# Side products and evictions of a decoder layer filed between four parts of each slab, and the indexer keys filed ahead of the decays

## The reference

```python
h = rms_norm(x, attn_norm_g)
proj = h @ w_in                  # hq hf hi hg cq ak av ik iw gate_a gate_b
oa = hgrn2_mixer(hq, hf, hi, lb)           # gated recurrence, 4 heads of 128
oa = rms_norm(oa, hgrn_norm_g) * silu(hg)
cq = rms_norm(cq, q_norm_g)
aq, iq = cq @ w_uq, cq @ w_iq
ik = layer_norm(ik, idx_k_norm_g, idx_k_norm_b)
ob = dsa_mixer(aq, iq, iw, ak, av, ik, rel_bias)
mix = sigmoid(gate_a) * (oa @ w_up_hgrn) + sigmoid(gate_b) * (ob @ w_up_attn)
x = x + mix @ w_o                # then the MLP and a last RMSNorm
```

## Time and profile before

| | us |
|---|---|
| three runs | 774.33, 774.77, 776.5 |
| median | 774.77 |
| profiled execution, own time | 774.76 |
| its span in the trace | 773.0 |
| PE busy | 735.1 |
| DVE busy | 549.0 |
| ACT busy | 353.4 |
| POOL busy | 85.3 |

### The profile page before, as it was taken

The page is one execution under the profiler, slowest core; times in us unless marked ns, Lnnn a source line. Parts: engine busy times, 40 slices in busy tenths (PEclk is TensorE's granted clock), DMA queues, the critical chain, the costliest instruction groups (busy, mean ns, idle before and its releaser), DMA issues.

```text
span 773.0 us, 9939 instructions
## 1 busy us (share of the span) xinstructions
PE 735.1 (95%) x3498; PEld 608.7 (79%) x3498; DVE 549.0 (71%) x868; ACT 353.4 (46%) x571; POOL 85.3 (11%) x121
## 2 busy tenths in 40 slices
PE   5999998896998999999999999999999999999995
PEld 4788887785876788888888878878787878787884
DVE  5587997758999886434833686776869595968964
ACT  6463445465443344433321754635354444445441
POOL 5021330010001244400200100000000000000003
PEclk9999999999999999999999999999999999999998
DMA  7421221201231121112350624140505142332002
GB/s 283 158 89 56 81 82 55 83 28 54 83 109 55 56 81 56 55 54 83 119 209 27 218 81 137 55 163 24 187 6 167 50 138 79 109 109 86 23 1 109
DMA packets 20724, 71.51 MB, mean 92 GB/s; under 512 B 2344, under 2 KB 3536, under 8 KB 20688
## 3 DMA queue, kind: packets, MB, share of 16 engines
q1 hardware_dynamic: 19120, 67.88, 25.7%
q10 hardware_dynamic: 1568, 3.15, 1.2%
HBM read 68.91 MB, written 2.11 MB: 92 GB/s over the span
## 4 chain that ended last, share of the span: by engine, by line
PE 72%; DVE 17%; issue 5%; ACT 3%; DMA 1%; POOL 1%; DVEq 0%; SPq 0%; POOLq 0%; ACTq 0%
PE bank L1432 21%; PE bank L1434 21%; PE bank L1433 21%; DVE sc L1103 2%; PE bank L1655 2%; DVE small L1100 2%; DVE wlo L946 2%; DVE acc L1312 2%; PE bank L1440 1%; DVE wlo L1279 1%; PE bank L1559 1%; DVE al L1304 1%; DMA xs<-x 1%; ACT whi L860 1%; DVE sc L1090 1%
## 5 line engine op out<-in xcount | busy, mean ns | idle before, releaser
L1432 PE MATMUL bank<-hTh,whi 128*128 128x512 f32 (+1 forms) x456 | 181.1, 397 | 1.5 <-DVE hTl L966 1.5
L1433 PE MATMUL bank<-hTl,whi 128*128 128x512 f32 (+1 forms) x456 | 178.7, 392 | 0.0
L1434 PE MATMUL bank<-hTh,wlo 128*128 128x512 f32 (+1 forms) x456 | 178.6, 392 | 0.0
L1432 PEld LDWEIGHTS bank<-hTh,whi 128*128 128x128 f32 (+1 forms) x456 | 86.1, 189 | 21.2 <-issue 3.0
L946 DVE TENSOR_TENSOR wlo<-raw,whi 128x1024 fp32r<-128x1024 f32 x58 | 72.2, 1246 | 42.0 <-ACT whi L630 42.0
L1434 PEld LDWEIGHTS bank<-hTh,wlo 128*128 128x128 f32 (+1 forms) x456 | 85.9, 188 | 18.7
L1433 PEld LDWEIGHTS bank<-hTl,whi 128*128 128x128 f32 (+1 forms) x456 | 85.9, 188 | 18.2 <-issue 0.5
L1432 PE MATMUL bank<-whi,ah 128*128 128x512 f32 x196 | 77.8, 397 | 2.1 <-DVE acc L1312 2.1
L1434 PE MATMUL bank<-whi,al 128*128 128x512 f32 x196 | 76.4, 390 | 0.0
L1433 PE MATMUL bank<-wlo,ah 128*128 128x512 f32 x196 | 76.4, 390 | 0.0
L630 ACT CAST whi<-raw 128x1024 fp32r<-128x1024 f32 x58 | 60.4, 1044 | 34.7 <-PE bank L1434 34.5
(11 more groups left out here) (227 smaller groups left out, 1396.8 us busy)
## 6 DMA issues: line engine op xcount, KB each, us to landing
raw<-slabs SPq DMA_DIRECT2D x87, 512.0 KB, 3.3
br<-slabs SPq DMA_DIRECT2D x32, 512.0 KB, 3.3
xs<-x SPq DMA_DIRECT2D x4, 512.0 KB, 5.6
y<-x ACTq DMA_DIRECT2D x1, 2048.0 KB, 9.2
out<-ys SPq DMA_DIRECT2D x3, 512.0 KB, 2.6
bt<-bias_rows ACTq DMA_DIRECT2D x1, 1024.0 KB, 5.3
cst<-consts SPq DMA_DIRECT2D x1, 608.0 KB, 9.1
fg<-final_g SPq DMA_DIRECT2D x1, 512.0 KB, 7.3
```

Source lines behind the costliest of these rows:

```text
L1432: pe.matmul(dst, lh, rh, start=start, stop=False)
L1433: pe.matmul(dst, lh, rl, start=False, stop=False)
L1434: return pe.matmul(dst, ll, rh, start=False, stop=stop)
```

## The change

Each slab is cut into four parts of six matmuls, and the side steps and evictions are filed between them. `woven[n][p]` holds the steps that follow part p: the steps with PE products are spread evenly over the four parts (one goes after the third, two after the second and fourth, three after the first, third and fourth), and steps without a product stay behind the one that they follow. Evictions of part p stand ahead of these steps, for kinds by token and for iq and uq one bank in each part; `EARLY` goes. `cqT`, `kdT` and the other key steps are filed ahead of `decay_k`, `use_k` and `decay_q`, `turn` ahead of `use_q`; `ikd` and `ikh` get space of their own (197.5 and 195, which held the bias rows until they were written out), DVE's wait on `kk_done` goes, ACT waits on `scr_done` (the bias rows' write) instead, and `ikl` is made in `kdT`, not in iq's eviction.

```diff
-        ikd = place("ikd", 165, T)
-        ikh = place("ikh", 167, T, F32R)
+        ikd = place("ikd", 197.5, T)
+        ikh = place("ikh", 195, T, F32R)
...
-        file(n_de - 1, ("decay_k",))
-        file(n_de, ("put", LEVELS - 1), ("use_k",), ("decay_q",))
-        file(n_de + 1, ("use_q",), ("turn",))
         file(n_hi, ("ikT",))
         file(n_hi + 1, ("prep",))
         file(n_hi + 2, ("cqT",))
         file(n_hi + 3, ("kdT",))
+        file(n_de - 1, ("decay_k",))
+        file(n_de, ("put", LEVELS - 1), ("use_k",), ("decay_q",))
+        file(n_de + 1, ("turn",), ("use_q",))
...
-        EARLY = (n_hi + 3, n_iq, n_uq, n_hg + 3)
...
+        PARTS = 4
+        woven = {}
+        for n in range(NPLAN):
+            woven[n] = [[] for _ in range(PARTS)]
+            count = sum(s in BK for s in side[n])
+            seen, p = 0, 0
+            for s in side[n]:
+                if s in BK:
+                    p = (2 * seen + 1) * PARTS // (2 * count)
+                    seen += 1
+                woven[n][p].append(s)
...
                 hi(n + AHEAD)
-                if n in EARLY:
-                    evict(n)
-                for s in side[n]:
-                    do_side(s)
-                if n not in EARLY:
-                    evict(n)
+                for p in range(PARTS):
+                    evict(n, p)
+                    for s in woven[n][p]:
+                        do_side(s)
...
                     b, u = BK[s][2]
+                    act.wait_ge(S["scr_done"], 16)
                     act.wait_ge(free[b], u + 1)
                     act.activation(ikh[:, :], ikd[:, :], ACT.Copy).then_inc(S["ikh_done"], 1)
...
                     wait_full((b, u))
-                    dve.wait_ge(S["kk_done"], 1)
                     dve.tensor_scalar(ikd[:, :], bank[b][:, :], vec[:, V_IKG:V_IKG + 1], vec[:, V_IKB:V_IKB + 1],
                                       ALU.mult, ALU.add).then_inc(free[b], 1)
+                    dve.wait_ge(S["ikh_done"], 1)
+                    dve.tensor_tensor(ikl[:, :], ikd[:, :], ikh[:, :].bitcast(F32), ALU.subtract).then_inc(S["ikl_done"], 1)
...
-                if kind == "ua":
-                    for q, (b, u) in enumerate(tiles[n]):
-                        m = 2 * j + q
+                if kind == "ua" and p % 2:
+                    q = p // 2
+                    b, u = tiles[n][q]
+                    m = 2 * j + q
...
             for n in range(NPLAN):
-                mms(n)
-                for s in side[n]:
-                    do_side(s)
+                for p in range(PARTS):
+                    mms(n, p)
+                    for s in woven[n][p]:
+                        do_side(s)
```

## The result

The changed kernel takes 778.43 us in the median of 8 runs (777.69 to 778.8). The kernel before, run 8 times beside it, takes 775.62 us (773.92 to 777.59). The ratio is 1.0036 with a 95% interval of 1.0024 to 1.0049. I had forecast 771.6, with 766.5 to 777.5 as the range: the sign was wrong, and the time lies above the range. It lies where rival C stood, 778.5.

The account below looks back on a forecast made before the run. PE was taken to bound most stretches, DVE's queue 170 to 281 us. Terms −0.75 − 2.35 + 0.3 − 0.4 = −3.2 took 774.8 to 771.6 us, range 766.5 to 777.5.

Parts of the forecast that it names:

- rival C: Three-head slabs 29, 30, 32, 33: fourth quarter left behind ob's wait at lower clock, +1.8 each; 778.5 us; chance 0.20.
- What bounds the kernel: Whole order to 424 us: PE to 125, ACT/DVE chain to 138.5, PE to 170, DVE's queue to 281, then PE.
- Part 1: Slabs 0 to 15: side products a quarter slab earlier, +0.5 us on PE; GpSimd's price only changes bearer, 0.
- Part 2: Keys and iq, slabs 15 to 18 (120 to 148 us): later iq evictions delay PE, +1.1 us.
- Part 3: hg1 to uq (148 to 200 us): rounds earlier, −0.75 with part 2 included; DVE's slab 22 wait gone, −2.35.
- Slab 28: Start of attention: DVE arrives 3.1 us early, PE waits some 4 to 6 us instead of about 1; no price.
- Part 4: Attention, slabs 28 to 34 (234 to 281 us): slower heads and lower clock against filled gaps, +0.3 us taken.
- Part 5: 281 to 424 us, PE-bound: heads move but don't grow, one wait of 0.47 us goes, −0.4 us.
- A: Rival, 170 to 281 us: the weave fills 3/4 of DVE's gaps too; 766.5 us; chance 0.17.

Follow-up runs that it names:

- x1: Changed kernel, but in slabs 28 to 34 side products and evictions stand behind the whole slab; 771.25 us, ratio to before 0.9946.
- x3: Changed kernel with slabs 29 and 30 alone put back to their sides behind the whole slab; 775.08 us, ratio to before 0.9989.
- x5: Changed kernel with PE's idle waits in slabs 28 and 29 filled by 20 and 16 matmuls without a result; 774.76 us, ratio to before 0.9993.
- x13: x1 with ACT's wait for the last out product put back ahead of uq's first quarter; 771.17 us, ratio to before 0.9939.
- x9: Kernel before with only ACT's wait for the last out product moved to uq's third quarter of evictions; 772.34 us, ratio to before 0.9968.
- x2: Changed kernel with slab 28 alone put back to its sides behind the whole slab; 775.0 us, ratio to before 0.9994.
- x10: x5 with two more waits filled, 12 matmuls in slab 30 and 8 in slab 32; 773.31 us, ratio to before 0.9972.
- x8: Changed kernel, new key order kept, with only slabs 18 to 22 woven and all others whole; 770.29 us, ratio to before 0.9931.
- x6: x1 with slabs 16 to 18 whole too, use_k and decay_q filed behind iq's evictions; 768.27 us, ratio to before 0.9915.
- x11: x6 with only slabs 19 to 22 woven, all others whole; 768.25 us, ratio to before 0.9904.

## Why the prediction was wrong, point by point

- **What bounds the kernel**: right. DVE's lead at 200 us (3.7) is kept to 234 us without loss, and with x1's order to the end.
- **Part 1** (+0.5 on PE, 0 for GpSimd's price): slab 16 begins on PE at 120.77, before at 120.86, and PE has no idle time from 43 to 120 us. So the +0.5 did not come, nor the 121.7 from which part 2 starts. GpSimd's subtraction now falls beside `wlo` in two slabs (2.32 and 2.78 us instead of 1.25 and 1.21), and the multiplies that took 2.91 us take 1.22: the price stays in the main, with another bearer. This is also what the Trainium skill, "SBUF — State Buffer", "Who interferes with whom", would have: `wlo` too has two inputs in SBUF.
- **Part 2** (+1.1): right in nearly every step. The fourth `hV` ended at 134.8 (forecast 135.5), PE waited 2.02 us there (2.3), the last `iqs` pair ended at 144.0 (144.6), slab 19 began at 148.47 (148.6). One wait is not where I had it. I wrote that PE would reach the first indexer product at 142.0 and wait until 144.6. In this execution PE got there at 144.43 and waited for nothing, since the twelve matmuls ahead of it ran at 0.50. In the profiles of x3 and x5, whose lower stretch is half as long there, the wait is 1.22 and 1.25 us, and the product begins at 144.62 and 144.85. So the last `iqs` pair bounds it as forecast, and the lower clock only takes the wait's place. Here are the two waits of PE in the changed kernel:

```profile
134.88 0.44 PE L1439 MATMUL bank<-cqh,whi 128*128 128x384 f32 x1 [2.02 <-ACT hV L708]
...
138.32 0.77 PE L1439 MATMUL bank<-whi,hTh 128*128 128x512 f32 x1 [2.12 <-DVE iqs L1001]
```

- **Part 3** (−3.1 together): right, and a little small. The rounds began at 169.69 (169.6), `aqs` on DVE at 185.44 without a wait, the lead was 3.7. What I had missed is a second reason: I gave the gain of slab 22 to the weave, which x13 bears out, but the change also moves ACT's wait for the last `out` product, and that alone gives the gain too (x9).
- **Slab 28**: the step that failed first. I wrote that PE would wait there some 4 to 6 us, and it waited 4.8; but I put no price on it and gave no reason for that. I missed that the weave leaves 18 of the 24 matmuls behind that wait, and with them the second head (behind twelve) and the third (behind all 18), for which DVE then waits. Price 2.9 us; x2 and the table show it, x10 shows that 0.1 is left at full clock.
- **Part 4, slabs 29 to 34** (+0.3): the mechanism was right and its size wrong. I took +0.7 for DVE's heads in slabs 29 and 30; at full clock they were +0.9 and +1.2. I took one stretch at the lower clock at 1.1 us and counted half of it; it came behind three of PE's four waits, in slabs 28, 29 and 32, and cost 1.8 us in slab 29 and 1.0 in slab 32 (x10 against after). Of the 1.6 us that the `tha` evictions and the shorter wait were to give in slabs 31 to 33, slab 31 gave 1.0; slabs 32 and 33 lost 1.3 and 0.4.
- **Part 5** (−0.4): the wait of 0.47 us is gone, yet 0.4 were lost from slab 35 on. Why stays open: between x1, where the heads from slab 35 on are woven, and x8, where they aren't, the profiles differ by 0.1 us there.
- **The sum**: against the forecast, parts 1 to 3 came 0.6 better (3.7 for 3.1), slab 28 cost 2.9 where I had nothing, slabs 29 to 34 4.5 where I had 0.3, and slab 35 on +0.4 where I had −0.4. That is 7.3, and the span moved by +4.0 where I had −3.2.
- **The chances**: rival C has the mechanism, and its 778.5 is in part luck. It counts 1.8 us in each of slabs 29, 30, 32 and 33, 7.2 in all. Measured were 2.7, 1.2, 1.3 and 0.4, together 5.6; slab 28, which is not in C, adds 2.9, and slab 31 gives 1.0 back. The sign that I had named for C, gaps on DVE of 1.5 us and more in slabs 31 to 33, did not show: the longest there is 1.37. I gave C 0.20 since before the change one wait of PE of 1.76 us had not been followed by the lower clock, and I cut the range through the middle of it. The row that spoke for C was in my own list: 0.98 us of work in 3.3 us, and then 0.50. The change makes such waits longer, since PE comes to them earlier: 4.0 us instead of 2.26. I should have counted such a stretch for each of the long ones. The low end of the range had a slip as well: A's sum leaves out the +1.1 that its sentence names, and with it A stands at 767.6.

## What to carry to other kernels

When side work is filed between the parts of a large step, first ask of each piece whether it can wait, and what then stands behind it: independent work belongs ahead of a product that may wait, not behind it. When an engine wins time that the engine it waits for does not win, its later waits grow: in slab 28 PE's wait for the heads' sums on DVE is 1.2 us before, 3.0 in x9 and 3.3 in x1. And a long idle wait of PE can be paid a second time, in the clock of what follows it. Look for single waits that stand earlier than their reason: one moved line gave 2.5 us here, over half of what x8 gave with the keys and five woven slabs (4.6).

## What the runs showed of the hardware

- The lower clock mostly follows PE's long waits: 4.8 us idle, then 0.50 until 233.6; 4.0 us idle, then 0.50 until 250.4. Behind shorter ones it may or may not come: behind 1.8 us in slab 32 it came in the changed kernel and not in x2, whose 2.66 us in slab 30 it did not follow either; behind 2.84 us ahead of hg0 it came in x6 and not in x11. At 0.50 the pitch of 512-column matmuls is 0.43 us (245.56 after 245.13), at full clock 0.2275 (before the change, slab 19: 24 matmuls begin from 147.51 to 152.74).
- Matmuls without a result kept the clock at 1.00 where it falls to 0.50 when the same waits are left unfilled (x5 and x10). With four of them filled in slabs 28 to 32, 5.1 us came back without any change of order (778.43 to 773.31; 5.0 by the ratios).
- The spread between runs of one kernel goes in part with the mean clock. Before the change, in the last group, the runs of 773.65 to 774.87 have a mean clock of 0.989 to 0.990 and those of 775.61 to 776.4 have 0.986; x11 has 0.995 and 0.989. Not everywhere: x1's runs of 770.98 and 772.84 both have 0.987. A difference of 2 us between two medians of few runs can be only that. The Trainium skill, "TensorE: Matmul & The Clock Gate", Part 1, calls the effect variable from run to run, and these runs agree.
